# Squares of two norms summed on VectorE ahead of the products of ones, in the gate stage of a per-layer embedding

## The reference, cut to what matters

```python
def rmsnorm(x, g):
    xf = x.astype(jnp.float32)
    y = xf * lax.rsqrt(jnp.mean(xf * xf, axis=-1, keepdims=True) + EPS)
    return (y * g.astype(jnp.float32)).astype(x.dtype)

def ple_add(h, p_i, g, w_gate, b_gate, w_proj):
    gate = jax.nn.sigmoid(rmsnorm(h, g) @ w_gate + b_gate)
    return h + gate * (p_i @ w_proj)
...
            h = ple_add(h, p[i], g_ple[i], w_ple_gate[i], b_ple_gate[i], w_ple_proj[i])
            if i == N_A - 1:
                kv = shared_kv(h, g_kv_in, w_dkv, g_kv_lat, w_kr, pos)
        return rmsnorm(h, g_final), jnp.stack(conv_new), kv[0], kv[1]
```

## Time and profile before

| what | value |
|---|---|
| device time, three runs | 1478.04, 1477.97, 1475.92 us; median 1477.97 us |
| profiled execution | 1475.82 us, of which the span is 1474.0 us |
| busy: PE, PEld | 1168.8 us (79%), 762.2 us (52%) |
| busy: DVE, ACT, POOL | 501.3 us (34%), 319.5 us (22%), 24.9 us (2%) |
| gate's products, L1836 | 256 instructions, 62.8 us |
| DMA | 464.11 MB, mean 315 GB/s |

### The profile page before, as it was taken

The page is one execution under the profiler, slowest core; times in us unless marked ns, Lnnn a source line. Parts: engine busy times, 40 slices in busy tenths (PEclk is TensorE's granted clock), DMA queues, the critical chain, the costliest instruction groups (busy, mean ns, idle before and its releaser), DMA issues. The chain is left out here.

```text
span 1474.0 us, 25393 instructions
## 1 busy us (share of the span) xinstructions
PE 1168.8 (79%) x10817; PEld 762.2 (52%) x10817; DVE 501.3 (34%) x1392; ACT 319.5 (22%) x821; POOL 24.9 (2%) x33
## 2 busy tenths in 40 slices
PE   8999896948659576799978988997876857766787
PEld 7767653525335343477655646664443524433456
DVE  4972611222122121243855541522121212212134
ACT  4573231101101000142233330231110101101123
POOL 0100000000000000001011100000000000000000
PEclk9999998978869687899999996998887968878899
DMA  8644399999999999963044317459999999999950
GB/s 266 207 199 178 130 426 428 426 425 429 426 428 425 428 424 425 414 217 115 0 152 179 130 65 296 189 233 427 426 427 426 425 427 429 425 428 422 425 218 30
DMA packets 61164, 464.11 MB, mean 315 GB/s; under 512 B 17533, under 2 KB 28826, under 8 KB 35423
## 3 DMA queue, kind: packets, MB, share of 16 engines
q1 hardware_dynamic: 58830, 442.95, 72.8%
q0 software_dynamic: 1792, 18.88, 3.5%
q10 hardware_dynamic: 416, 0.53, 0.1%
HBM read 460.80 MB, written 2.49 MB: 314 GB/s over the span
## 5 line engine op out<-in xcount | busy, mean ns | idle before, releaser
L982 PE MATMUL ps<-area,hiddenT 128*32 128x256 f32 x2304 | 189.3, 484 | 201.8 <-issue 200.4
L982 PEld LDWEIGHTS ps<-area,hiddenT 128*32 128x32 f32 x2304 | 88.6, 134 | 283.3 <-issue 258.6
L1668 DVE COPY y<-ps 32x256 f32<-32x256 f32 x144 | 60.0, 417 | 425.4 <-PE ps L982 424.2
L972 PE MATMUL ps<-area,uT 128*32 128x256 f32 x2560 | 166.8, 416 | 38.5 <-DMA area<-in_w_exp_up_dram 20.4
L972 PEld LDWEIGHTS ps<-area,uT 128*32 128x32 f32 x2560 | 95.3, 121 | 107.3 <-issue 44.4
L1606 ACT COPY y<-ps 32x256 f32<-32x256 f32 x144 | 52.6, 366 | 383.2 <-PE ps L982 382.3
L972 PE MATMUL ps<-area,xsT 128*32 128x256 f32 x2048 | 125.9, 400 | 0.0
L1332 PE MATMUL ps<-sel,u_rows 128*128 128x256 f32 (+3 forms) x480 | 124.6, 386 | 0.4 <-DVE sel L1304 0.4
L1720 DVE TENSOR_TENSOR hidden<-silu,ps 128x128 f32<-128x128 f32 x72 | 20.7, 288 | 281.3 <-ACT silu L1622 281.3
L972 PEld LDWEIGHTS ps<-area,xsT 128*32 128x32 f32 x2048 | 75.6, 118 | 49.4 <-issue 14.3
L1332 PEld LDWEIGHTS ps<-sel,u_rows 128*128 128x128 f32 (+1 forms) x480 | 77.1, 187 | 44.9 <-issue 35.1
(11 more groups left out here) (370 smaller groups left out, 1254.1 us busy)
## 6 DMA issues: line engine op xcount, KB each, us to landing
area<-in_w_exp_gate_dram SPq DMA_DIRECT2D x64, 2048.0 KB, 21.6
area<-in_w_exp_up_dram SPq DMA_DIRECT2D x64, 2048.0 KB, 26.1
area<-in_w_exp_down_dram SPq DMA_DIRECT2D x64, 2048.0 KB, 23.5
area<-in_conv_w_in_dram SPq DMA_DIRECT2D x8, 1024.0 KB, 11.6
area<-in_w_ple_gate_dram SPq DMA_DIRECT2D x2, 4096.0 KB, 34.8
area<-in_conv_w_out_dram SPq DMA_DIRECT2D x1, 4096.0 KB, 19.0
area<-in_w_o_dram SPq DMA_DIRECT2D x1, 4096.0 KB, 12.9
area<-in_w_uq_dram SPq DMA_DIRECT2D x3, 768.0 KB, 10.7
```

The source lines that it names most:

```text
L972: last = pe.matmul(s.ps[SLOT * j:SLOT * (j + 1), bank, 0:2 * P].rearrange("p (a f) -> p a f", a=2), xT[:, k, :], up[:, :, k, j * P:(j + 1) ...
L982: last = pe.matmul(s.ps[SLOT * g:SLOT * (g + 1), bank, 0:q], hidden[:, SLOT * j:SLOT * (j + 1)], down[:, j, g * q:(g + 1) * q], start=(j = ...
L1668: last = V.tensor_copy(y[a:a + SLOT, (e // PER) % 2, g * q4:(g + 1) * q4], s.ps[SLOT * g:SLOT * (g + 1), 3 + e % 2, 0:q4])
```

## The change

Where TensorE added the eight chunks of squares by eight products of ones, VectorE now adds squares, element by element, and TensorE sums over partitions once or twice.

First norm: ScalarE squares the eight chunks at the beginning of the gate stage (activation `Square`), VectorE adds them in a chain of seven additions into `rstd`, and one product of ones follows gate chunk 0. The squares that VectorE made in the experts' stage are gone.

Second norm: VectorE squares chunk c - 1 after it has scaled chunk c, and from c = 2 adds the square into that of chunk 0, while ScalarE takes the sigmoid. TensorE issues two products of ones at the end, one of the sum over chunks 0 to 6 and one of chunk 7's squares. `followed` keeps only the transposes.

```diff
@@ -1649,11 +1649,6 @@
                     V.tensor_tensor(s.hT[:, c, :], s.ps[:, 6 + c % 2, 0:T], s.hT[:, c, :], ALU.add)\
                         .then_inc(s.added.sem, 1)
 
-                def square(c):
-                    dve.wait_ge(s.added.sem, s.added.at(DC * (quads - 1) + c + 1))
-                    V.tensor_tensor(ple_views(s).squares[:, c, :], s.hT[:, c, :], s.hT[:, c, :], ALU.mult)\
-                        .then_inc(s.squared.sem, 1)
-
                 def choose(i):
                     dve.wait_ge(s.xs_mm.sem, s.xs_mm.at(i * pairs))
                     halves = select(nc, s, m.sel[:, :, :], m.rel, i * TOPK * 3)
@@ -1735,9 +1730,6 @@
                     copy_out(e)
                 for c in range(DC):
                     add(quads - 1, c)
-                    if c:
-                        square(c - 1)
-                square(DC - 1)
         for k in range(UPS):
             s.up_in[k].ended(32 * len(range(k, E, UPS)))
         for k in range(DOWNS):
@@ -1756,7 +1748,6 @@
         s.ple_out.ended(DC)
         s.ple_proj_in.ended(16)
         s.gained.ended(DC)
-        s.squared.ended(DC)
         s.diag_ready.ended(2)
         s.wide_mm.ended(2)
         s.wide_out.ended(2 * TOPK)
@@ -1837,9 +1828,8 @@
                                        start=(k == 0), stop=(k == DC - 1))
                     mm.then_inc(s.proj_mm.sem, 1)
 
-                def sum_of(c):
-                    return pe.matmul(s.ps[:, sums, 0:T], s.ones[:], v.squares[:, c, :], start=(c == 0),
-                                     stop=(c == DC - 1))
+                def sum_of(rows, start, stop):
+                    return pe.matmul(s.ps[:, sums, 0:T], s.ones[:], rows, start=start, stop=stop)
 
                 def turn_rows(c):
                     for i, (t0, n) in enumerate(TILES[0:2]):
@@ -1851,24 +1841,23 @@
                                  col(s, "ident")).then_inc(s.rows_turned.sem, 1)
 
                 def followed(c):
-                    pe.wait_ge(s.squared.sem, s.squared.at(c + 1))
-                    mm = sum_of(c)
-                    if c == DC - 1:
-                        mm.then_inc(s.sums.sem, 1)
                     if last:
                         pe.wait_ge(s.gained.sem, s.gained.at(c + 1))
                         turn_rows(c)
 
                 pe.wait_ge(s.ple_in.sem, s.ple_in.at(16))
                 gate_products(0)
-                for c in range(DC):
-                    mm = sum_of(c)
-                mm.then_inc(s.sums.sem, 1)
+                pe.wait_ge(s.summed.sem, s.summed.at(DC - 1))
+                sum_of(s.rstd[:], True, True).then_inc(s.sums.sem, 1)
                 for c in range(1, DC):
                     gate_products(c)
                     if c >= 2:
                         followed(c - 2)
                 followed(DC - 2)
+                pe.wait_ge(s.summed.sem, s.summed.at(2 * DC - 3))
+                sum_of(v.squares[:, 0, :], True, False)
+                pe.wait_ge(s.squared.sem, s.squared.at(1))
+                sum_of(v.squares[:, DC - 1, :], False, True).then_inc(s.sums.sem, 1)
                 followed(DC - 1)
                 if last:
                     pe.wait_ge(s.rooted.sem, s.rooted.at(2))
@@ -1878,6 +1867,8 @@
 
             @block.scalar
             def _(act):
+                for c in range(DC):
+                    nc.scalar.activation(v.squares[:, c, :], s.hT[:, c, :], ACT.Square).then_inc(s.squares_act.sem, 1)
                 act.wait_ge(s.sums.sem, s.sums.at(1))
                 root(nc, s, s.rstd, sums, D).then_inc(s.rooted.sem, 1)
                 for c in range(DC):
@@ -1908,6 +1899,16 @@
             def _(dve):
                 V = nc.vector
                 link = chained(dve, s.dve)
+                def square(c):
+                    dve.wait_ge(s.proj_out.sem, s.proj_out.at(c + 1))
+                    return V.tensor_tensor(v.squares[:, c, :], s.hT[:, c, :], s.hT[:, c, :], ALU.mult)
+
+                for c in range(1, DC):
+                    dve.wait_ge(s.squares_act.sem, s.squares_act.at(c + 1))
+                    if c > 1:
+                        dve.wait_ge(s.summed.sem, s.summed.at(c - 1))
+                    V.tensor_tensor(s.rstd[:], s.rstd[:] if c > 1 else v.squares[:, 0, :], v.squares[:, c, :], ALU.add)\
+                        .then_inc(s.summed.sem, 1)
                 dve.wait_ge(s.rooted.sem, s.rooted.at(1))
                 V.reciprocal(s.rstd[:], s.rstd[:]).then_inc(s.inverted.sem, 1)
                 dve.wait_ge(s.inverted.sem, s.inverted.at(1))
@@ -1915,13 +1916,19 @@
                     dve.wait_ge(s.proj_mm.sem, s.proj_mm.at(c + 1))
                     V.tensor_tensor(gate[:, c % 2, :], s.ps[:, c % 2, 0:T], s.rstd[:], ALU.mult)\
                         .then_inc(s.scaled.sem, 1)
+                    if c:
+                        link(square(c - 1))
+                    if c > 1:
+                        if c > 2:
+                            dve.wait_ge(s.summed.sem, s.summed.at(DC + c - 4))
+                        V.tensor_tensor(v.squares[:, 0, :], v.squares[:, 0, :], v.squares[:, c - 1, :], ALU.add)\
+                            .then_inc(s.summed.sem, 1)
                     dve.wait_ge(s.acted.sem, s.acted.at(c + 1))
                     link(V.tensor_tensor(gate[:, c % 2, :], gate[:, c % 2, :], m.proj[:, c, :], ALU.mult))
                     V.tensor_tensor(s.hT[:, c, :], s.hT[:, c, :], gate[:, c % 2, :], ALU.add)\
                         .then_inc(s.proj_out.sem, 1)
-                    dve.wait_ge(s.proj_out.sem, s.proj_out.at(c + 1))
-                    V.tensor_tensor(v.squares[:, c, :], s.hT[:, c, :], s.hT[:, c, :], ALU.mult)\
-                        .then_inc(s.squared.sem, 1)
+                square(DC - 1).then_inc(s.squared.sem, 1)
+                s.n_link = link.made[0]
                 if last:
                     dve.wait_ge(s.pe.sem, s.pe.at(1))
                     V.reciprocal(per_row[:, 0:2], s.ps[:, 0, 0:2 * P:P])
@@ -1951,11 +1958,13 @@
         s.scaled.ended(DC)
         s.acted.ended(DC)
         s.gained.ended(DC)
-        s.squared.ended(DC)
+        s.squared.ended(1)
+        s.summed.ended(2 * DC - 3)
+        s.squares_act.ended(DC)
         s.sums.ended(2)
         s.rooted.ended(2 if last else 1)
         s.inverted.ended(2 if last else 1)
-        s.dve.ended(DC)
+        s.dve.ended(s.n_link)
 
 
 
```

## The result

The changed kernel took 1466.38 us in the median of six runs (1464.58 to 1470.76 us), the kernel before 1476.72 us (six runs, 1473.81 to 1478.04 us). The ratio is 0.9938, with an interval from 0.9923 to 0.9953. The forecast was 1465.3 us and 11.64 us off the profiled execution; that of the changed kernel took 1466.33 us, 9.49 us less. By the medians it is 10.34 us.

A forecast was written before the change was run, and what follows sets the result against it. DMA bounds the experts, TensorE's products the gate stages. Per layer 3.11 + 2.22 + 0.63 - 0.14 = 5.82 us, twice 11.64 us, gives 1464.2 us from the profile or 1466.3 us from the median; forecast 1465.3 us, range 1461.5 to 1469.5 us.

The forecast's parts named there:

- The products of ones: Gate stage, TensorE: 0.445 us each on the path; seven go in the first norm, five in the second, per layer.
- 3.11 + 2.22 - 0.14: Per gate stage: 3.11 us from the first norm's products, 2.22 us from the second's, less 0.14 us at the last chunk.
- VectorE's longer chunk: Second norm: about 2 us of VectorE work per chunk, hidden under TensorE's 3.56 us except at the last chunk.
- The end of the experts: Without squares, VectorE's additions follow TensorE alone and the stage ends 0.63 us earlier per layer.
- The additions' chain: First norm: seven dependent additions, starts 0.47 us apart, end 4.1 us into the gate stage, 1.0 us ahead of need.
- The clock at the beginning: Both gate stages begin with TensorE at half speed, chunk 0 in 5.48 us; this was forecast to stay.
- both drops: The falls of TensorE's clock to 1.2 GHz at the beginning of each layer's gate stage, chunk 0 taking 5.48, not 3.56 us.
- The rival with clock gains: One or both early clock drops at the gate stages go: 1.0 to 2.0 us more gained, 1463 to 1464.5 us; chance 0.09.
- Signs of being wrong: TensorE waits for the seven additions, VectorE's chunk holds back a gate chunk, or 5.8 us miss the second experts' start.
- the first layer's 5.8 us: The first layer's gain, forecast to appear whole as an earlier start of the second layer's experts.
- The work between the layers: From the first gate stage's end to the second layer's experts: forecast to start 5.8 us earlier, the saturated stretch moving as much.
- Theory B: From the experiments: moving the work between the layers regularly brings half-speed stretches there; 2.5 us given back in layer 0's forecast.

The follow-up runs named there:

- squares_kept: The changed kernel with VectorE's squares, unused, still in the experts' stage; ratio 0.9952 to the kernel before.
- second_norm_only: The kernel before with only the second norm's part of the change, in both layers; ratio 0.9981 to the kernel before.
- two_chains: The changed kernel with the first norm's additions split into two interleaved chains; ratio 0.9909 to the kernel before, 1463.61 us.
- shift_by_four_products: The kernel before with four more products of ones, result overwritten, ahead of the first norm's eight in the first layer; ratio 1.0002.

## Why the prediction held, point by point

**The products of ones were on the path, and their price was right.** The terms without a change of clock were 3.11 + 2.22 - 0.14 = 5.19 us per gate stage; squares_kept measured 5.21 us where the beginning stayed at half speed, and second_norm_only 2.09 us for 2.22 - 0.14. VectorE's longer chunk held no gate chunk back.

**The end of the experts** was put at 0.63 us. The segment is 216.86 to 216.93 us in all kernels without the squares and 217.49 to 217.58 us in all with them: 0.6 to 0.7 us, though the loads keep the DMA engines busy until shortly before. In the first layer, from the last products of L982 to chunk 0, it was 9.74 us before (623.11 to 632.85 us) and 9.11 us after (624.13 to 633.24 us).

**The additions' chain** was mis-sized: 0.47 us apart was read from instructions with one wait (L1919, L1920), and these additions have two. The chain of the changed kernel shows the second as a piece of its own (L1909), which ends with the addition before:

```profile
1422.08 0.45 DVE rstd L1910
...
1422.55 0.02 DVEq L1909
1422.57 0.05 issue
1422.62 0.44 DVE rstd L1910
```

They started 0.54 us apart, the sum was ready 4.47 us after the beginning and not 4.1 us. At half speed chunk 0 still covers it, as in the first layer of squares_kept, where TensorE did not wait.

**The clock at the beginning** is the step that failed: "The change shortens the loose part and leaves the gap; I keep both drops." Both went. The gap was put at 1.4 us, from the start of the last addition; TensorE's own row has 1.60 us, and it did not stay but went to 1.32 us. The rival with clock gains had this at 1.0 us per layer; with the longer chain it was 0.74 us.

**Signs of being wrong.** Of the three that the prediction named, two came. TensorE waited 0.68 us for the seven additions. And of the first layer's 5.8 us only 2.9 us appear in the start of the second layer's experts, here the third load of their gate weights, in the kernel before and in the changed one:

```profile
941.09 0.34 SPq L948 DMA_DIRECT2D area<-in_w_exp_gate_dram  x1
```

```profile
938.15 0.34 SPq L948 DMA_DIRECT2D area<-in_w_exp_gate_dram  x1
```

**The work between the layers** was taken to move as a whole. It moved, but from the page table to the third load of the second layer's expert weights it took 2.6 us longer in the changed kernel's profile, and 0.35 us less and 4.0 us more in its two repetitions. Theory B, that the earlier start costs this every time, falls: two_chains begins this work as early as the changed kernel, and takes 69.67 us as the kernel before. That it costs it more often is not excluded: nine of the eleven profiles with a shorter gate stage 1 lost clock there, and neither of the two with the old one. The shift does not decide it either, since shift_by_four_products moved it the other way and lost 1.26 us. What decides in which execution the clock falls there stays open.

**The sum of the profile.** 2 x 5.95 us in the gate stages and 0.66 us at the second experts' end make 12.56 us; 2.62 us was given back between the layers, 0.39 us up to the first gate stage and about 0.05 us elsewhere. That leaves the 9.5 us of the two spans. The 0.39 us hold the first layer's own 0.63 us at the experts' end, so the unchanged work ahead took 1.0 us more in this execution; the first gate stage begins between 632.8 and 637.7 us over the fourteen profiles. The forecast of 11.64 us was near partly by luck: the clock's gain and loss, 1.5 us for the two beginnings against 2.6 us between the layers, go against each other, and the forecast had neither. The same program measured 9.2, 12.5 and 12.6 us in three sets of runs (0.9938 and twice 0.9915). The Trainium skill's rule that activity releases the throttled state ("TensorE: Matmul & The Clock Gate", "What's actually happening") is in line with the granted 1.00 in 19 of 19 beginnings behind the closer products.

## What to carry to other kernels

A sum over partitions by products of ones costs a product for each chunk on the engine that is the bound; adding the chunks first on an idle engine leaves one, and here its price could be read off the chain of waits to within 0.02 us per stage, as long as nothing waited for the sum. A dependent chain on VectorE is paid by the distance of its starts (0.54 us here, 0.34 us for additions that do not depend on one another), so two interleaved chains shorten the stage once the cover shrinks. And work just ahead of a dense stretch of products can have a part in the clock at which the stretch begins.

## What the runs showed of the hardware that was not expected

Eight squares less on VectorE, beside the last products of the experts, went with full speed at the beginning of the next stage: 3.80 us for chunk 0 in 19 of 19 beginnings, against 5.47 to 5.49 us in seven of nine with the squares. And one program ran the same 278 matmul instructions of the segment between in 65.80, 65.81 and 68.27 us of busy TensorE, at a granted 0.98, 0.98 and 0.94; the kernel before took 64.55 us at 1.00.
